# Splitting the feature-major input projections of a hybrid decoder block into 128-column matmuls

## What is computed

```
h    = RMSNorm(x)
proj = h @ w_in            # 1024 -> 2576 columns: q, k, v, low rank, gates, pool, memory query
gla  = chunked gated linear attention of q, k, v (4 heads, chunks of 64), head RMSNorm, * silu(gate)
pool = causal mean pooling (windows 2, 4, 8, 16) minus token, per-group linear, * silu(gate)
mem  = cross-attention of the memory query into 256 memory tokens, * silu(gate)
y    = RMSNorm_final(x + concat(gla, pool, mem) @ w_out)
```

## Time and profile before

| | us |
|---|---|
| two runs | 1544.86 and 1545.45, median 1545.15 |
| span of the profiled execution, first to last instruction | 1543.8 |
| time of the runs that lies outside such a span | about 1.35 |

### The profile page before, as it was taken

One profiled execution on the slowest core, in us unless ns is written; L12 is line 12 of the kernel. 1 busy time (PEld: TensorE's weight loads), 2 busy tenths in 40 slices (PEclk: granted clock), 3 DMA queues, 4 the chain that ended last, 5 costly groups with the idle time before them and its releaser, 6 DMA issues.

```text
span 1543.8 us, 28261 instructions
## 1 busy us (share of the span) xinstructions
PE 1443.0 (93%) x11746; PEld 1046.2 (68%) x11746; DVE 724.0 (47%) x1221; ACT 608.1 (39%) x1101; POOL 236.4 (15%) x217
## 2 busy tenths in 40 slices
PE   3359699999999999999999999999999999999996
PEld 2238476776867677676867677686867767686762
DVE  2876625436172535527163544627163543616253
ACT  1344425344342534434252534434262534434241
POOL 1231201121110201121020202121020112112000
PEclk9669799999999999999999999999999999999998
DMA  8130100102010010102001010202001010201001
GB/s 337 65 136 1 42 2 28 54 0 82 0 69 12 27 54 10 71 0 82 0 36 46 27 54 0 82 0 82 0 27 54 21 61 0 82 0 46 10 28 68
DMA packets 15432, 69.32 MB, mean 45 GB/s; under 512 B 2352, under 2 KB 2480, under 8 KB 12848
## 3 DMA queue, kind: packets, MB, share of 16 engines
q1 hardware_dynamic: 15408, 68.98, 11.9%
HBM read 52.20 MB, written 16.78 MB: 45 GB/s over the span
## 4 chain that ended last, share of the span: by engine, by line
PE 90%; DVE 4%; ACT 2%; DMA 1%; issue 1%; POOL 1%; SPq 1%; DVEq 0%; ACTq 0%; POOLq 0%
PE bank L330 75%; PE bank L484 2%; PE bank L452 2%; PE bank L490 2%; PE bank L476 2%; PE bank L498 2%; DVE whl L852 1%; PE bank L541 1%; DVE wmx L816 1%; PE bank L463 1%; PE bank L388 1%; DMA whl<-in_pool_w 1%; PE bank L435 1%; PE bank L380 1%; POOL arena L1134 1%
## 5 line engine op out<-in xcount | busy, mean ns | idle before, releaser
L330 PE MATMUL bank<-arena,whl 128*128 128x256 f16 x6144 | 684.6, 274 | 2.6 <-DVE whl L852 2.6
L330 PEld LDWEIGHTS bank<-arena,whl 128*128 128x128 f16 x6144 | 602.3, 98 | 84.1 <-issue 6.5
L330 PE MATMUL bank<-arena 128*128 128x512 f16 x1536 | 344.1, 381 | 6.4 <-DVE arena L872 6.4
L330 PEld LDWEIGHTS bank<-arena 128*128 128x128 f16 x1536 | 147.8, 98 | 181.3 <-issue 15.4
L963 DVE SCALAR_TENSOR_TENSOR arena<-arena 64x256 f32<-64x256 f32 x60 | 25.2, 420 | 314.6 <-POOL arena L1191 313.2
L330 PE MATMUL bank<-whl,arena 128*128 128x512 f16 x768 | 168.3, 379 | 0.0
L686 ACT ACTIVATE arena<-bank,sca 128x512 f32<-128x512 f32 x64 | 43.9, 688 | 254.4 <-PE bank L330 253.3
L330 PEld LDWEIGHTS bank<-whl,arena 128*128 128x128 f16 x768 | 75.2, 99 | 86.9
L1143 POOL TENSOR_TENSOR arena<-arena 128x1024 f16<-128x1024 f32 x32 | 77.8, 2451 | 285.7 <-ACT arena L621 285.7
L1134 POOL TENSOR_TENSOR arena<-arena 128x1024 f32<-128x1024 f32 (+2 forms) x48 | 76.7, 1599 | 231.7 <-ACT arena L599 222.6
L1184 POOL TENSOR_TENSOR arena<-arena 128x542 f32<-128x542 f32 x16 | 17.4, 1090 | 606.1 <-ACT arena L693 598.3
(11 more groups left out here) (154 smaller groups left out, 1467.9 us busy)
## 6 DMA issues: line engine op xcount, KB each, us to landing
arena<-in_xt SPq DMA_DIRECT2D x16, 1024.0 KB, 5.2
arena<-in_x SPq DMA_DIRECT2D x32, 512.0 KB, 3.3
out<-arena SPq DMA_DIRECT2D x32, 512.0 KB, 2.6
arena<-in_w_in SPq DMA_DIRECT2D x8, 768.0 KB, 16.1
arena<-in_w_out SPq DMA_DIRECT2D x1, 4096.0 KB, 12.2
arena<-in_w_in SPq DMA_DIRECT2D x8, 392.0 KB, 16.2
arena<-in_w_mem SPq DMA_DIRECT2D x1, 2048.0 KB, 11.0
arena<-in_memt SPq DMA_DIRECT2D x1, 1024.0 KB, 6.6
```

The source lines that it names most:

```text
L330: mm = nc.tensor.matmul(ap, lhs, rhs, start=k == 0 and n == 0, stop=(k, n) == last)
```

## The change

`features` no longer calls `split`. It writes the same loops out, and each matmul of 256 token columns becomes two of 128, one for each half t of the block. Both have the same stationary tile, which is loaded for each of them. The two write to columns `j * TB + t * P` on of the bank. The order over j, k and the three products stays. `start`, which clears the marks of written columns in the whole bank, is now given once for the bank, at its first matmul, and no more at the first of j = 1. With `arriving`, the wait for the weight tile stands once for each k, no more once for each matmul. All else in the kernel stays as it is.

```diff
             def features(b, c0, arriving=False):
 
-                def parts(k, p, r, c):
-                    if arriving:
-                        wait_split(pe, k)
-                    return whl[:, p, k, c:c + P], xn[:, r, k, :]
-
                 for j in range(2):
-                    mm = split(bank[b][:, j * TB:(j + 1) * TB], KT,
-                               lambda k, p, r, c=c0 + j * P: parts(k, p, r, c))
+                    c = c0 + j * P
+                    for k in range(KT):
+                        if arriving:
+                            wait_split(pe, k)
+                        for n, (p, r) in enumerate(((0, 0), (0, 1), (1, 0))):
+                            for t in range(NT):
+                                o = j * TB + t * P
+                                mm = nc.tensor.matmul(bank[b][:, o:o + P], whl[:, p, k, c:c + P],
+                                                      xn[:, r, k, t * P:(t + 1) * P],
+                                                      start=j == 0 and t == 0 and k == 0 and n == 0,
+                                                      stop=k == KT - 1 and n == 2, skip_group_check=True)
                 return mm
```

## The result

The changed kernel takes 1564.07 us in both of its runs, against a median of 1545.15 us before. The ratio is 1.0126, with a 95% interval of 1.0109 to 1.0142: clear of noise, slower, and under 2%. The forecast was 14.7 us more; it became 18.9. The profiled execution has a span of 1562.6 us, 18.8 more than before.

What follows compares the result with a forecast made beforehand. TensorE, never idle in the middle, was taken to bound the kernel; 6144 pairs at 2.4 ns more add 14.7 us to a 1543.8 us span, 1558.5, plus 1.35 around it: forecast 1560 us, range 1545 to 1580.

Steps and rivals of the forecast that it cites:

- The path: Middle of the kernel: TensorE busy 1209.00 of 1209.00 us, so every nanosecond of longer matmul sequence goes to the end.
- The price of a pair: Feature matmuls: two of 128 columns cost 111.6 ns in place of 109.2; 6144 pairs add 14.7 us.
- Loads cost nothing: The 6144 added weight loads of 98 ns lie beside matmuls on TensorE and were costed at nothing.
- The Trainium skill's 81 ns: Sustained distance of matmuls with their own loads at 128 columns: a pair would take 162 ns, the kernel 1869 us.
- loads not hidden: Rival: in long feature runs loads can't hide behind 128 columns; 2078 us at a full 98 ns a matmul; chance 0.05.
- First rival, instructions loaded again: TensorE's loop no longer stays loaded: 9 packets a block, 1573 us if only jumps show it, 1686 if all; chance 0.09.
- Second and third rival: Second: loads can't hide behind 128 columns, 2078 us, 0.05; third: same tile and bank pays no surcharge, 1545 us, 0.05.
- The small parts: First-block waits, lower clock level, single `start`, next-token wait and other engines' work: each taken as about nothing.
- The wait for the next tokens: The loop's wait for the low part of the next tokens: about a microsecond to spare, and the margin stays.
- The first block: Its wait is made 16 times in place of 48; at most 2 us could be saved, taken as 0.
- the lower clock level: At 1.2 GHz the surcharge may vanish for some 100 of the 6144; under 0.3 us.

Runs made afterwards that it cites:

- the runs of 64 columns: Changed kernel with every feature matmul made four of 64 columns, same tile loaded four times: 1600.01 us, 1.0356 of the kernel before.
- the halves apart: Changed kernel with all matmuls of one half of the tokens first, then all of the other half: 1563.78 us, ratio 1.0122.

## Why the prediction was right

*The path.* TensorE without a free moment in the middle, so that each nanosecond counts: confirmed, since blocks grew by the pairs' cost and nothing absorbed any of it.

*The price of a pair.* Taken as 111.6 ns from runs of 16 transposes, measured as 111.68 in runs of up to 576. The surcharge of 2.5 ns now stands at 64, 128, 256 and 512 columns (29.17, 55.84, 109.19 and 215.8 ns). It made some 15 of the 18.9 us: 15.3 by count, of which 0.4 did not show in the first block. The forecast had 14.7.

*Loads cost nothing.* Right for 12288 float16 loads and wrong for two float32 loads a block, which I did not look at: the term counted what lies over the new loads, but not what the shorter matmuls leave over the old load behind them. It was put at 0 and measured at 0.11 us a block, 1.7 us. This is one of the two missing terms of the sum; the other is the clock at the ends of the run, below.

*The Trainium skill's 81 ns* for sustained matmuls of 128 columns with their loads ("TensorE: Matmul & The Clock Gate", section "Back-to-back issue gap"): the traces disagree, with 55.84 ns in runs of 576 on this chip and 29.17 ns for half the columns. The prediction gave this rule no chance of its own; its 1869 us could only fall under "loads not hidden", at 0.05, and it was right to keep that low on the strength of the failure at 512 columns.

*First rival, instructions loaded again.* I gave it 0.09 as a cause of loss. Its mechanism happened with certainty, 10 packets a block where I had counted 9, and its cost was nothing in the changed kernel. What decided was not in my list for and against: what is queued ahead of the jump. The sentence that the jumps alone would cost 13 us had a jump at 1 us; it is 3.5 us, and where it is open the loss was 41 us. This rival was to show as packets in the middle of the run and as gaps: the packets came and the gaps did not, so the forecast held although half of the sign against it appeared. That the jump stood where it was covered was luck, since the prediction had not asked where it stands.

*Second and third rival.* Both are out, by the runs of 64 columns and by the halves apart.

*The small parts.* The wait for the next tokens kept its margin, 1.6 us where it was 1.1. The first block gave back some 0.4 us where the prediction had 0; whether by fewer waits or otherwise is open. What the lower clock level might do was put at under 0.3 us in favour, and it was 2.0 us against.

*A slip.* The prediction says that runs of 96 would take about 10.6 us and runs of 576 about 64 us. At its own 55.8 ns they are 5.4 and 32.1 us, as measured; the forecast does not rest on that line.

## What to carry to other kernels

On an engine that never stops, price a split by the distance between starts in a long run and by the number of matmuls added, and look at each matmul that follows a shortened one for a load longer than its new cover. Then count the instructions of the loop body: above what stays loaded, the jump back went from 0.2 to 3.5 us here, and whether that costs anything depends on the work queued where the loop happens to be cut. Cut it behind long matmuls, or name its target ahead, which left 2.6 us once at the end of the loop.

## What was not expected of the hardware

- A 128x128 float16 load is recorded with 98 ns, yet one was taken up every 29.17 ns over 1152 matmuls with no gap.
- A TensorE loop of some 1460 loads and matmuls ran with at most one instruction packet in 450 us, and one of some 1840 with 46.
- TensorE's jump back took 3.3 to 4.2 us once its loop was not kept, and 0.35 us with its target named a turn ahead. Code in straight stretches came without a gap at 28 ns an instruction. At 15 ns an instruction there was one gap of 0.35 us some 13 us behind each jump back, and none elsewhere.
- After five of twelve idle gaps of some 2.7 us, TensorE went on at the 1.2 GHz level for a while, at a cost of 8.8 us.
